# Thirteen instead of ten buffers for expert weights, three of them laid over tensors that are idle by then

## What is computed

```python
h  = rmsnorm(x, ln1_g) * (1 + sc1) + sh1
z  = h @ w_in                         # 1,024 x 3,600: conv | attention | mLSTM heads | gates
x  = x + g1 * concat(conv(z), attention(z, cache), mlstm(z, state)) @ w_out
h2 = rmsnorm(x, ln2_g) * (1 + sc2) + sh2
# 16 experts, each token goes to two of them
a  = silu(einsum('nd,edf->nef', h2, w_gate)) * einsum('nd,edf->nef', h2, w_up)
x  = x + g2 * einsum('nef,efd->nd', a * gates[..., None], w_down)
```

## Time and profile before

| | |
|---|---|
| median of 3 runs | 1252.42 us (1251.08 to 1258.88) |
| the profiled execution, its own time | 1253.02 us |
| its span, from the first instruction to the last | 1251.0 us |
| PE busy | 1150.2 us, 92% of the span, mean granted clock 0.972 |
| DVE, ScalarE (ACT), POOL busy | 408.6, 250.2 and 56.5 us |
| data moved | 315.15 MB, mean 252 GB/s |
| expert stage of layer 0 and layer 1, on PE | about 371 to 632 us and 969 to 1230 us |

### The profile page before, as it was taken

How to read it: one execution, slowest core, us unless ns; L and a number is a source line. 1 busy time by engine, 2 the same in 40 slices (tenths; PEclk the granted TensorE clock), 3 DMA queues, 4 the chain that set the end, 5 groups by cost and what they waited for, 6 DMA issues and landing times.

```text
span 1251.0 us, 15287 instructions
## 1 busy us (share of the span) xinstructions
PE 1150.2 (92%) x6240; PEld 625.5 (50%) x6240; DVE 408.6 (33%) x1148; ACT 250.2 (20%) x515; POOL 56.5 (5%) x82
## 2 busy tenths in 40 slices
PE   3999999898989998999999999998998999899886
PEld 3546555586544433453344565566654453355333
DVE  4402032355361333222252302225627033322324
ACT  2210122152141101111042011214313201011003
POOL 1500000000020000000010000000000000000001
PEclk8999999999989999999989999999998989999998
DMA  8966453275309989999971356234430898999991
GB/s 318 331 202 242 144 202 135 102 271 184 135 15 381 414 355 412 409 397 413 364 268 68 135 175 233 73 135 169 119 119 16 321 412 317 414 409 394 413 407 54
DMA packets 95512, 315.15 MB, mean 252 GB/s; under 512 B 5980, under 2 KB 6352, under 8 KB 86608
## 3 DMA queue, kind: packets, MB, share of 16 engines
q1 hardware_dynamic: 91856, 306.43, 64.1%
q0 software_dynamic: 3584, 7.71, 2.5%
HBM read 310.92 MB, written 4.99 MB: 253 GB/s over the span
## 4 chain that ended last, share of the span: by engine, by line
PE 78%; DMA 8%; DVE 8%; ACT 3%; issue 2%; SPq 0%; POOL 0%; DVEq 0%; POOLq 0%; ACTq 0%
PE ps L921 15%; PE ps L1318 15%; PE ps L931 8%; PE ps L1365 7%; DMA ring<-in_w_up 7%; PE ps L1089 6%; PE ps L1156 5%; PE ps L878 3%; PE ps L868 2%; PE ps L1184 2%; PE ps L1185 1%; PE ps L1208 1%; PE ps L1055 1%; DMA slot<-in_w_up 1%; PE ps L1120 1%
## 5 line engine op out<-in xcount | busy, mean ns | idle before, releaser
L1318 PE MATMUL ps<-ring,arena 128*64 128x512 f32 x816 | 231.9, 598 | 12.4 <-DMA ring<-in_w_up 12.2
L921 PE MATMUL ps<-ring,hT 128*128 128x512 f32 (+1 forms) x480 | 194.9, 565 | 0.0
L1985 DVE SCALAR_TENSOR_TENSOR xT<-ps,modT,xT 128x128 f32<-128x128 f32 x320 | 109.3, 410 | 216.6 <-PE ps L1185 128.3
L921 PEld LDWEIGHTS ps<-ring,hT 128*128 128x128 f32 x480 | 90.5, 190 | 98.0 <-issue 94.7
L1318 PEld LDWEIGHTS ps<-ring,arena 128*64 128x64 f32 x816 | 70.6, 137 | 125.8 <-issue 125.8
L1365 PE MATMUL ps<-ring,arena 128*64 128x512 f32 x384 | 116.7, 604 | 8.1 <-ACT arena L1648 8.1
L931 PE MATMUL ps<-hT,ring 128*128 128x384 f32 x320 | 106.2, 489 | 0.0
L1318 PE MATMUL ps<-slot,arena 128*64 128x512 f32 x208 | 100.9, 606 | 4.2 <-DMA slot<-in_w_up 4.2
L1089 PE MATMUL ps<-mixT,ring 128*128 128x384 f32 x256 | 84.0, 489 | 1.7 <-ACT mixT L1576 1.7
L931 PEld LDWEIGHTS ps<-hT,ring 128*128 128x128 f32 x320 | 59.8, 190 | 40.7 <-issue 0.8
L2209 DVE SCALAR_TENSOR_TENSOR y_low<-ps,route,y_high 128x512 fp32r<-128x512 f32 x32 | 24.0, 751 | 171.5 <-ACT y_high L1654 170.8
(11 more groups left out here) (322 smaller groups left out, 1206.3 us busy)
## 6 DMA issues: line engine op xcount, KB each, us to landing
ring<-in_w_up SPq DMA_DIRECT2D x56, 1024.0 KB, 9.9
ring<-in_w_gate SPq DMA_DIRECT2D x54, 1024.0 KB, 13.4
ring<-in_w_down SPq DMA_DIRECT2D x52, 1024.0 KB, 9.6
ring<-in_w_mod SPq DMA_DIRECT2D x24, 2048.0 KB, 11.8
ring<-in_w_in SPq DMA_DIRECT2D x14, 2048.0 KB, 11.5
slot<-in_w_down SPq DMA_DIRECT2D x16, 1024.0 KB, 10.3
slot<-in_w_gate SPq DMA_DIRECT2D x14, 1024.0 KB, 13.1
slot<-in_w_up SPq DMA_DIRECT2D x12, 1024.0 KB, 7.9
```

The lines of the kernel that those rows point to most:

```text
L921: mm = pe.matmul(p[:, 0:n], hT[:, k, t * P:(t + 1) * P], w[:, k, c0:c0 + n], start=(k == 0), stop=(k == KT - 1))
L1318: mm = pe.matmul(out[which][64 * s:64 * s + 64, :], xg[:, k, cols[s]], w[i][:, k % 4, :], start=(k == 0), stop=(k == KT - 1))
L1985: ins = dve.scalar_tensor_tensor(xT[:, m, cols], p[:, cols], modT[:, L, gate0 + m, j:j + 1], xT[:, m, cols], ALU.mult, ALU.add)
```

## The change

Three slots are added, so that a chunk `n` goes into slot `n % 13` or `(n + 6) % 13`. Slot 10 lies over `vaug` (the mLSTM values) and `upad` (padded input of the convolution), which is moved next to it; slot 11 over `relb` and half of `gbc` (a norm weight); slot 12 over `caug` and `cnew` (old and new mLSTM state). In layer 1 what was overwritten is made again: DVE sets `upad` and the column of ones in `vaug` at the start of the layer, and POOL loads `gbc`, `state_C` and `relb` for layer 1 after the last reads of slots 11 and 12 in layer 0, where before it loaded them after the routing. The semaphores `chunk_loaded` are now shared by the layers, with counts that go on. The slots of the fixed job move from 4 to 9 to 11, 12, 0, 1, 2, 3. The branch `n == 13` in `first_free` is never reached, since that function is called for `n < SLOTS` alone.

```diff
-SLOTS = 10
+SLOTS = 13
...
     def wait_chunk_loaded(self, eng, n):
         slot = slot_of(n)
-        eng.wait_ge(self.chunk_loaded[slot], 16 * sum(slot_of(i) == slot for i in range(n + 1)))
+        before = self.number * sum(slot_of(i) == slot for i in range(STATIC))
+        eng.wait_ge(self.chunk_loaded[slot], 16 * (before + sum(slot_of(i) == slot for i in range(n + 1))))
...
         vaug = sb("vaug", [P, 3, 4, 129])
+        upad = sb("upad", [P, 2, 388])
         arena = sb("arena", [P, 6668])
-        upad = sb("upad", [P, 2, 388])
...
-                 ring_half(3, 0), ring_half(3, 1), ring_half(0, 0), ring_half(0, 1)]
+                 ring_half(3, 0), ring_half(3, 1), ring_half(0, 0), ring_half(0, 1),
+                 over("slot10", "vaug", 0, [P, CHUNK], F32)[:], over("slot11", "relb", 0, [P, CHUNK], F32)[:],
+                 over("slot12", "caug", 0, [P, CHUNK], F32)[:]]
...
                 def first_free(n):
...
+                    elif n == 10:
+                        bk.wait_full(sp, ("C", 7))
+                        sp.wait_ge(ly.conv_ready, 2)
+                    elif n == 11:
+                        sp.wait_ge(ly.hnorm_ready, 4 * ly.number + 1)
+                    elif n == 12:
+                        sp.wait_ge(ly.stored, 16 * 4)
...
                 load(cachev[:], a["cache_v"][0, d].rearrange("t h d -> t (h d)"))
-                load(caug[:, :, 0:P], a["state_C"][0, d].rearrange("r h d e -> d (r h) e"))
-                load(gbc[:], a["ml_norm_g"][d:d + 1].broadcast_to((P, 512)))
                 load(wroute[:, :, 0:4], a["w_rg"][d].rearrange("(k p) n -> p k n", p=P))
...
                 load(rbias[:, 4:20], a["b_re"][d:d + 1].broadcast_to((P, 16)))
+                if not ly.first:
+                    for slot in (11, 12):
+                        layers[d - 1].wait_chunk_read(pool, max(n for n in range(STATIC) if slot_of(n) == slot))
+                load(gbc[:], a["ml_norm_g"][d:d + 1].broadcast_to((P, 512)))
+                load(caug[:, :, 0:P], a["state_C"][0, d].rearrange("r h d e -> d (r h) e"))
...
(ACT, by_feature)
+                    if i == 4 and not ly.first:
+                        act.wait_ge(pads_ready, 1)
...
(DVE, start of a layer)
+                if not ly.first:
+                    layers[L - 1].bk.wait_full(dve, ("y", PAIRS - 1, 1))
+                    dve.memset(upad[:], 0.0)
+                    dve.memset(vaug[:, :, :, 128:129], 1.0).then_inc(pads_ready, 1)
                 dve.wait_ge(ly.gates_loaded, 16 * GATE_LOADS)
```

More of the change, by code:

```diff
@@ L351, with __init__ @@
 class Layer:
-    def __init__(self, sem, number, ring_loaded, shared):
+    def __init__(self, sem, number, ring_loaded, chunk_loaded, shared):
         self.number = number
@@ L366, in __init__ @@
         self.mod_read = s("mod_read")
-        self.chunk_loaded = [s(f"chunk_loaded{r}") for r in range(SLOTS)]
+        self.chunk_loaded = chunk_loaded
         self.first_half_read = s("first_half_read")
@@ L479, in build @@
         shared = {name: sem(name) for name in SHARED_BY_LAYERS}
-        layers = [Layer(sem, n, ring_loaded, shared) for n in range(DEPTH)]
+        chunk_loaded = [sem(f"chunk_loaded{r}") for r in range(SLOTS)]
+        layers = [Layer(sem, n, ring_loaded, chunk_loaded, shared) for n in range(DEPTH)]
         xT = sb("xT", [P, KT, NT])
@@ L578, in build @@
         assert place["cb"] - place["kctx"] == 4 * CHUNK and place["cst"] - place["cb"] >= 4 * CHUNK
+        assert place["arena"] - place["vaug"] >= 4 * CHUNK
+        assert place["relb"] - place["caug"] >= 4 * CHUNK and place["vT"] - place["relb"] >= 4 * CHUNK
         def ring_half(r, upper):
@@ L624, in build @@
             sem(n) for n in ("set_once", "windows_written", "csil_ready", "vT_ready", "mod_ready"))
+        pads_ready = sem("pads_ready")
         dve_chain, act_chain, loop_chain = (sem(n) for n in ("dve_chain", "act_chain", "loop_chain"))
@@ L702, in first_free @@
                         sp.wait_ge(ly.kv_stored, 16 * 2)
+                    elif n == 10:
[5 more added lines that the diff above has]
+                        sp.wait_ge(ly.stored, 16 * 4)
+                    elif n == 13:
+                        if not ly.first:
+                            last = layers[ly.number - 1]
+                            last.wait_chunk_read(sp, max(n for n in range(STATIC) if slot_of(n) == 13))
                     else:
```

## The result

| | before | after |
|---|---|---|
| median of 4 runs each | 1253.86 us (1251.08 to 1258.88) | 1233.81 us (1233.55 to 1233.99) |
| ratio of the runs | | 0.9836, 95% interval 0.9802 to 0.9869 |
| the profiled execution, its own time | 1253.02 us | 1233.71 us |
| its span | 1251.0 us | 1231.9 us |

The account below looks back on a forecast made before the run. PE, busy 92% of the span, was held up by 16.4 us of chunk waits behind a DMA stream at full rate. 1253.0 - 7.6 - 7.75 = 1237.7 us, median 1237; forecast 1233 to 1240, range 1233 to 1245.

Parts of the forecast that it names:

- all that earlier weights can give directly: PE's waits for expert-weight chunks in both layers' expert stages: 16.4 us, claimed as the direct gain available.
- Layer 0, 7.6 us: Layer 0's expert stage: loses all its waits for chunks, 7.6 us, 0.9 of them ahead of the fixed job.
- The fall of the clock at 603 us: After layer 0's longest wait: PE's clock fall might go with the wait; taken as 0, bounds 1.8 us either side.
- Layer 1, 7.75 us: Layer 1's expert stage: of 8.8 us of waits, the lead of three chunks removes 7.75; upper bound 8.8.
- They take 7.75 us of idle DMA time: In the routing: chunks 10, 11 and 12 follow 8 and 9 at about 338 us, filling idle DMA time.
- the lead counts from the fixed job: In the fixed job buffers are full, now with three chunks more, so the 7.75 us lead counts from there.
- The late loads: `gbc`, `state_C`, `relb` issued near 603 us: 4.2 us of transfer, thinly covered; otherwise layer 0 gives back up to 4.2.
- part of the waits comes back: Rival: late loads compete with pair 7's chunks, costing 4.2 to 8 us; 1241 to 1245 us, chance 0.20.
- The memsets and the boundary: Start of layer 1: memsets cost nothing, bound 1.4 us; its later first load costs nothing, bound 3.5 us.
- The lead is lost in the fixed job: Rival: DMA stands 7.75 us longer in the job and old waits return behind it; 1252 us, chance 0.10.
- Slower: Rival: chunk 12 waits for layer state stores, delaying SP's stream; about 1283 us at 400 us landing, chance 0.06.
- The rest keeps its length: Outside the expert stages: each layer's remainder unchanged, while each expert stage gets 7 to 9 us shorter.

Follow-up runs that it names:

- the two complements: Kernel after with chunks 10 to 12 not early: ratio 0.9864, again 0.9855; kernel after with them early but later loads also awaiting their ten-slot reads: 0.9993.
- the run without the early start: Kernel after, but chunks 10 to 12 also wait until PE has read the first half of chunk 0: 1235.48 us, again 1233.77 us.
- the repeat of the change: Kernel after, unchanged, run again beside other kernels on the same chip: 1233.12 us, ratio 0.9841.
- the early start alone: Kernel after with chunks 10 to 12 early, but later chunks and job loads also wait for the read that freed their slot with ten: 1251.10 us.

## Why the prediction was right, and where it was not

**The kind of gain: right; its bound: somewhat low.** The waits for chunks fell from 16.4 to 1.3 us. But they were not "all that earlier weights can give directly": with the loads cut in half, layer 1's stage goes from 261.5 to 251.4 us, 10.1 us, where 8.8 us of waits are shown. PE's own pace between them, 26.5 us a pair, didn't change.

**Layer 0, 7.6 us: 7.9 measured, from parts that partly cancel.** The waits gave 7.6 - 1.1 = 6.5 us, since one wait in pair 7 stayed. The fall of the clock at 603 us, taken as 0 with 1.8 us as a bound, went with the wait in front of it, and groups of 24 matmuls take 5.15 (570.98 in the chain above) to 5.30 us, not 7.07: -1.8. Against it, the fall in the gather for the fixed job lasts longer (0.56 over the 7 us from 427 for 0.59 over four): the pair with the job takes 52.34 us for 50.84, +1.5. It begins in the gather's matmuls of 64 columns, and PE had stood idle 0.68 us in all in the 7 us ahead of it. This isn't the slots' doing: with ten slots and the small loads moved the same pair takes 52.32 us. The rest, about 1 us, is the next point.

**Layer 1, 7.75 us: this term was too small; 9.5 measured.** The waits gave 8.8 - 0.3 = 8.5, and the stage won more than the upper bound of 8.8, too. The lead was sized as three chunks at the rate of the long stretch, as if more slots couldn't change that rate. The run with eleven slots shows that they do: the short gaps go, and 7.75 + 1.5 = 9.2 us is nearly what was won. Counted by waits, 9.5 - 8.5 = 1.0 us is left here, as about 1 us is in layer 0: time that PE loses beside the waits that the view shows. Pair 6 of layer 0 is an example: from 565.65 to the next down product at 594.15 it took 28.50 us (its first row is among), where the same pair takes 26.54 after, and its one wait is 1.39. Of the other 0.57 us, 0.3 lie between the down product and the next gate product (7.22 us from start to start for 6.92), where no wait is shown; 0.16 more is the way a wait is counted, since matmuls overlap: one pair starts 0.43 us behind the other while each is shown with 0.59. About 0.1 is left. In layer 1 before, the stage stood 10.0 us above its floor of 251.5 with 8.8 us of waits shown.

**"They take 7.75 us of idle DMA time" in the routing: wrong as the cause, though it happened.** Without that time the kernel is as fast within about 2 us (0.9855 for 0.9841 on one chip), and with that time alone nothing is won (0.9993). The sentence behind it, that the lead counts from the fixed job, where full now means three chunks more, is what the runs bear out. Both sentences gave the same number, so the result could not tell them apart; the two complements did. That the number came out although the first sentence named the wrong source was luck.

**The late loads: hidden, as costed.** POOL issued them at 606 us, 3 us later than worked out, and each took longer to land than before, `relb` 13.7 us for 8.1; now all three run beside the chunk stream. POOL in order of time in the kernel after, then the DMA issues from 605 to 625 us (KB, us to landing), and then those of the kernel before from 366 to 386 us:

```profile
606.19 0.54 POOL L787 DMA_DIRECT2D gbc<-in_ml_norm_g  x1 [229.08 <-PE ps L1340]
606.72 0.90 POOL L787 DMA_DIRECT2D caug<-in_state_C  x1
607.61 0.55 POOL L860 DMA_DIRECT2D relb<-bias_windows  x1
```

```profile
relb<-bias_windows POOLq DMA_DIRECT2D x1, 896.0 KB, 13.7
caug<-in_state_C POOLq DMA_DIRECT2D x1, 512.0 KB, 11.7
gbc<-in_ml_norm_g POOLq DMA_DIRECT2D x1, 256.0 KB, 6.8
```

```profile
caug<-in_state_C POOLq DMA_DIRECT2D x1, 512.0 KB, 4.9
gbc<-in_ml_norm_g POOLq DMA_DIRECT2D x1, 256.0 KB, 4.8
```

They share the engines with the stream, as the Trainium skill ("DMA: Bandwidth & Descriptors", section "Issuing engines are not separate DMA queues") says; the trace agrees: beside the stream 256 KB took 6.8 us for 4.8 and 512 KB 11.7 for 4.9. But no wait at the down product followed. The one wait left in pair 7 ended at 607.2 us, 1 us after the first of them was issued, so at most that much of it can be theirs; the run without the early start has a wait of about the same length in pair 7, the repeat of the change has none. The rival "part of the waits comes back" therefore fell.

**The memsets and the boundary: nothing, as costed.** DVE in order of time in the kernel after:

```profile
634.65 0.70 DVE L1967 MEMSET upad<- 128x776 f32 x1 [0.42 <-DVE xT L2013]
...
635.32 0.07 DVE L1968 MEMSET vaug<- 128x12 f32 x1
...
638.72 2.55 DVE L1771 RECIPROCAL std<-std 128x384 f32<-128x384 f32 x1 [3.13 <-ACT std L1460]
```

0.77 us fit into an idle time that shrank from 4.30 to 3.13. PE's filling work behind layer 0 takes 3.43 us where it took 4.05.

**"The lead is lost in the fixed job": part of its sign came, its loss didn't.** In layer 0 the DMA engines do stand 2 us longer there (6.2 for 4.2), as the prediction had named for being wrong. The job itself lasts 1.5 us longer, by the clock. Both are so with ten slots and the small loads moved, too (6.4 us), so they don't come from the slots. But behind it the buffers hold three chunks more, and PE doesn't meet the old waits again: a stand of a resource that is ahead, and stays ahead, is no loss.

**"Slower", through the stores of the state: not met.** Chunk 12 went out with its neighbours at 340 us.

**"The rest keeps its length": not quite.** Outside the expert stages the profiled span is 1.7 us shorter, +1.4, -2.3 and -0.8, and 0.2 us more lies outside the span. The granted clock falls at other places there (a fall at 778 us is missing, one at 35 us is new, each worth some 1.7 us). In the profiles the part between the stages is 336.1 to 336.6 us with ten slots, 336.9 with eleven, 334.3 to 335.8 with twelve to fourteen, 336.3 with thirteen and the early start alone, 337.6 and 337.9 with thirteen and no early start. Whether the change has a part in this isn't shown; what moves these falls stays open.

Together, against the 15.35 us of the sum: 1.75 more in layer 1, 0.3 in layer 0, 1.7 outside, 0.2 around the span, 3.95 in all, which is 19.3 us and the 1233.7 us measured. So the time fell in the forecast of 1233 to 1240 us, but at its lower edge, and almost half of the distance from 1237 lies outside the stages, where nothing had been forecast.

**What stays open:** whether the fourteenth slot's 1.5 us is real, and why one fall of the clock follows a long wait while the falls in the fixed job's gather follow none.

## What to carry to other kernels

When a stream of loads and its consumer are nearly as fast as each other, find the last place ahead of the waits where the stream runs out of buffers: here the lead was set there, by the depth of the buffers and not by how early they were filled. Count a new buffer as one load's time, plus what the short gaps cost that it closes, and stop when the consumer's stage comes down to its length with the loads cut in half: here the stage of layer 1 went 261.5, 256.9, 254.1, 252.0 and 251.5 us over ten to fourteen slots, with 251.4 as its floor. To learn whether a prefetch or the depth behind it pays, run each without the other; the change alone can't tell.

## What the hardware showed that was not expected

A DMA share of 1.02 over 154 us doesn't mean that nothing was missing: two rows of 2 us at 0.96 and 0.83 lie inside it, and the stream moved 409 instead of 413 GB/s. Short stands show only in short stretches.

A wait of PE costs more than the trace shows as its length: 1.96 us for 1.39 in the pair worked out above, and 1.8 us more where the clock falls behind it. In the kernel before a wait of 2.19 us was followed by a fall and one of 2.00 us in layer 1 was not; with eleven slots waits of 2.03 and 2.25 us were. Part of those 1.8 us comes back: in all seven cases where the clock fell behind the long wait of pair 7, PE had no later wait in that stage; where it didn't fall, in the kernels with ten and twelve slots, one of 1.3 to 1.4 us came in the next group, as in layer 1 of the kernel before:

```profile
1211.90 3.65 PE L1318 MATMUL ps<-ring,arena 128*64 128x512 f32 x16 [1.31 <-DMA ring<-in_w_up]
```

While PE is short of weights the fall thus costs about 1.8 - 1.3 = 0.5 us net, an estimate. The Trainium skill ("TensorE: Matmul & The Clock Gate", section "HAM oscillation — how this bites in real kernels") describes a kernel in which each wait for DMA throttles the clock of the matmuls behind it; in the kernel before, one of the eleven waits did so. And a fall needs no wait for DMA: the one in the gather ahead of the fixed job is in the kernels before and after and in all the others, a granted clock of 0.56 with PE busy for 7.00 of 7 us.
